# Difference attention's heads kept unnormalised to its end, normalised by tokens beside the output projection; modulation blocks summed in halves

## What is computed

```python
# first block: four heads of difference attention, four of gated linear attention
p = softmax(s)                                   # two softmaxes per head, 64 features each
a = p[:, :, 0] - lam * p[:, :, 1]
da = rmsnorm(einsum(a, v), da_subln_w) * (1 - lam_init)     # norm over the 128 values of a head
go = rmsnorm(gla_bidirectional(...), gla_norm_w) * silu(gr)
h = h + concatenate([da, go]) @ w_out
# second block: both halves of the modulation, 12 blocks of 512 columns
mod, mod_c = silu(c) @ ada_w + ada_b, silu(c_ctx) @ ada_w[:, :2048] + ada_b[:2048]
```

## Time and profile before

| what | us |
|---|---|
| median of three runs | 2268.46 |
| profiled execution | 2262.53 |
| its span | 2261.2 |
| attention, first scores to first product of the output projection | 241.15 to 353.09 |
| output projection, to the residual's last tile on DVE | 353.09 to 395.37 |

### The profile page before, as it was taken

One profiled execution on the slowest core, in us unless ns is written; L12 is line 12 of the kernel. 1 busy time (PEld: TensorE's weight loads), 2 busy tenths in 40 slices (PEclk: granted clock), 3 DMA queues, 4 the chain that ended last, 5 costly groups with the idle time before them and its releaser, 6 DMA issues.

```text
span 2261.2 us, 31215 instructions
## 1 busy us (share of the span) xinstructions
PE 2109.3 (93%) x12667; PEld 1220.4 (54%) x12743; DVE 1524.8 (67%) x2558; ACT 890.9 (39%) x1066; POOL 713.0 (32%) x540
## 2 busy tenths in 40 slices
PE   6999889899999988999999999999789898999998
PEld 5464554455556646666665555555445464444444
DVE  4557664698889899998688888888674374432002
ACT  5333553333333336765433333333232454434110
POOL 2311001310333442232233333434336301555440
PEclk9999889999999999999999999999799998999999
DMA  5223552215988878899999999999422201322410
GB/s 207 75 75 114 197 203 83 84 49 195 330 307 299 333 274 300 332 353 341 372 373 378 376 382 377 382 382 374 174 75 98 75 20 38 112 83 104 149 38 37
DMA packets 194478, 483.37 MB, mean 214 GB/s; under 512 B 10672, under 2 KB 93648, under 8 KB 188320
## 3 DMA queue, kind: packets, MB, share of 16 engines
q1 hardware_dynamic: 154624, 334.65, 41.5%
q0 software_dynamic: 39712, 146.74, 17.2%
HBM read 428.92 MB, written 52.43 MB: 213 GB/s over the span
## 4 chain that ended last, share of the span: by engine, by line
PE 48%; DVE 29%; DMA 14%; issue 3%; ACT 3%; POOL 1%; SPq 1%; DVEq 0%; ACTq 0%; POOLq 0%
PE psum L565 13%; PE psum L566 13%; PE psum L564 13%; DMA expert_act<-act_dram 12%; DVE weight_low L2003 6%; DVE row_sum L2232 2%; POOL weight_low L2565 1%; DVE hidden_low L2411 1%; DVE gated_one_hot_b L2391 1%; DVE one_hot_b L2388 1%; DVE one_hot_a L2385 1%; DVE expert_act L2406 1%; DVE rows_a L2219 1%; PE psum L758 1%; PE psum L779 1%
## 5 line engine op out<-in xcount | busy, mean ns | idle before, releaser
L564 PE MATMUL psum<-x_high,weight_high 128*128 128x384 bf16 (+3 forms) x1826 | 630.0, 345 | 21.1 <-DVE weight_low L2003 15.7
L565 PE MATMUL psum<-x_low,weight_high 128*128 128x384 bf16 (+3 forms) x1845 | 637.2, 345 | 12.1 <-DVE x_low L1881 5.9
L566 PE MATMUL psum<-x_high,weight_low 128*128 128x384 bf16 (+3 forms) x1844 | 636.5, 345 | 0.6
L1289 ACT ACTIVATE weight_high<-weight_stage 128x4096 bf16<-128x4096 f32 (+2 forms) x100 | 356.3, 3564 | 240.8 <-PE psum L566 118.1
L2565 POOL TENSOR_TENSOR weight_low<-weight_stage,weight_high 128x512 bf16<-128x512 f32 (+1 forms) x229 | 299.5, 1341 | 422.7 <-ACT weight_high L1289 422.7
L564 PE MATMUL psum<-hidden_high,weight_high 128*128 128x384 bf16 x1024 | 333.8, 326 | 6.3 <-DVE hidden_low L2411 6.2
L566 PE MATMUL psum<-hidden_high,weight_low 128*128 128x384 bf16 x1024 | 333.8, 326 | 0.0
L565 PE MATMUL psum<-hidden_low,weight_high 128*128 128x384 bf16 x1024 | 333.8, 326 | 0.0
L2003 DVE TENSOR_TENSOR weight_low<-weight_stage,weight_high 128x4096 bf16<-128x4096 f32 x69 | 304.6, 4416 | 11.0 <-ACT weight_high L1289 11.0
L564 PEld LDWEIGHTS psum<-x_high,weight_high 128*128 128x128 bf16 (+1 forms) x1856 | 183.3, 99 | 183.1 <-issue 20.5
L566 PEld LDWEIGHTS psum<-x_high,weight_low 128*128 128x128 bf16 (+1 forms) x1856 | 183.4, 99 | 154.1 <-issue 7.0
(11 more groups left out here) (350 smaller groups left out, 2926.3 us busy)
## 6 DMA issues: line engine op xcount, KB each, us to landing
weight_stage<-peer_u_dram SPq DMA_DIRECT2D x32, 2048.0 KB
weight_stage<-peer_v_dram SPq DMA_DIRECT2D x32, 2048.0 KB
weight_stage<-mlp_w_dram SPq DMA_DIRECT2D x16, 2048.0 KB
weight_stage<-ada_w_dram SPq DMA_DIRECT2D x12, 2048.0 KB
act_dram<-norm_value SPq DMA_DIRECT2D x128, 192.0 KB
gate_dram<-gate_matrices SPq DMA_DIRECT2D x12, 2048.0 KB, 9.9
gates<-gate_dram SPq DMA_DIRECT2D x32, 768.0 KB
expert_act<-act_dram SPq DMA_DIRECT2D x32, 768.0 KB
```

What stands on the lines that cost most here:

```text
L564: self.nc.tensor.matmul(out, left[0], right[0], start=first, stop=False)
L565: self.nc.tensor.matmul(out, left[0], right[1], start=False, stop=False)
L566: return self.nc.tensor.matmul(out, left[1], right[0], start=False, stop=last)
L1289: nc.scalar.activation(k.block_view(m.w_high, n % SPLITS, n), k.block_view(m.w_stage, n % STAGES, n), ACT.Copy).then_inc(*s.w_high.up(n))
```

## The change

1. Difference-attention heads are copied from PSUM into four buffers and squared into buffers of linear attention that are free by then. Nothing else is done to them within the steps.
2. After the steps all four are normalised inside `mixer_out`. The sums of squares are taken with the squares as the stationary operand and two columns of ones (`token_sums`), so each token's sum is one value on one partition: 16 matmuls of two columns. One root of 128 x 16 values, one reciprocal of 128 x 16, then 16 matmuls of 128 columns spread them (`head_spread`), and DVE multiplies from PSUM.
3. `mixer_out` sums the four linear-attention features for tiles 0 to 3, with the sums of squares after tiles 0 and 1 and the spreads after tile 2; then the four difference-attention features for these tiles; then tiles 4 to 7 whole.
4. Linear-attention heads 2 and 3 are normalised in the same way, by 128 x 8 values, in steps 0 to 3.
5. Modulation blocks 4 to 9 are multiplied in halves of four matmuls in steps 4 to 15, blocks 10 and 11 whole in steps 16 and 17, the last turn is in step 18. Turns use bank 5, the sums bank 7.
6. The table of roots is loaded in step 16 (`root_table`).

```diff
 def ada_step(n):
-    g = ADA_LATE + n // 2
-    return (g - 1, None) if n % 2 == 0 and g <= 12 else (None, g) if n % 2 and g < 12 else (None, None)
+    if n == 0:
+        return ADA_LATE - 1, None, ()
+    if 4 <= n < 16:
+        g, half = ADA_LATE + (n - 4) // 2, n % 2
+        return g - 1 if half == 0 and g > ADA_LATE else None, g, (half,)
+    if n >= 16:
+        return (n - 7, n - 6, (0, 1)) if n < 18 else (n - 7, None, ())
+    return None, None, ()
...
 # PE
+    def token_sums(self, heads, stage, first, end, bank):
...
+        for h in range(first, end):
+            nc.tensor.wait_ge(*s.squared.at(stage, h))
+            square = k.head_square(stage, h)
+            for x in range(QT):
+                at = 2 * (QT * (h - self.first_head) + x)
+                ins = nc.tensor.matmul(k.psum[:, bank, at:at + 2], square[:, P * x:P * (x + 1)], self.m.ones[:, 0:2],
+                                       start=True, stop=True)
+        ins.then_inc(*s.square_sum.up(heads, end - 1))
+
+    def head_spread(self, stage, h, roots, bank):
...
+        for x in range(QT):
+            ins = nc.tensor.matmul(k.psum[:, bank, P * x:P * (x + 1)], roots[:, x:x + 1].to_broadcast([P, P]),
+                                   self.m.ident[:, :], start=True, stop=True)
+        ins.then_inc(*s.spread.up(stage, h))
...
-            part = gla_norm_part(GLA_SLOTS + n)
-            if part and part[1] == 1:
-                self.head_sum(("gla_head", part[0]), (7,))
-            part = da_norm_part(n, 1)
-            if part and part[1] == 1:
-                self.head_sum(("da_head", part[0]), (7,))
+            if n == 1:
+                self.token_sums("gla_heads", "gla_head", 2, GLA_HEADS, 7)
+            if n == 2:
+                nc.tensor.wait_ge(*s.inverted.at("gla_heads"))
+                for p in range(2):
+                    self.head_spread("gla_head", 2 + p, m.gla_roots[:, p, :], 6 + p)
             if n >= 3:
                 applying(n - 3)
-            turn, block = ada_step(n)
-            if turn is not None or block is not None:
-                self.modulation(turn, block, (7,))
+            turn, block, halves = ada_step(n)
+            if turn is not None:
+                self.modulation_turn(turn, (5,))
+            if block is not None:
+                self.modulation_sums(block, halves, (7,))
...
-        for t in range(6):
+        for t in range(4):
             banks.append(self.take(("w_out", t), (s.added, ("w_out", t)), (t,)))
-            part(t, order[:-1])
+            part(t, order[:4])
+            if t == 0:
+                self.token_sums("da_heads", "da_head", 0, DA_HEADS - 1, 7)
             if t == 1:
-                self.head_sum(("da_head", DA_HEADS - 1), (7,))
-        for t in range(6):
-            part(t, order[-1:])
-        for t in range(6, KT):
+                self.token_sums("da_heads", "da_head", DA_HEADS - 1, DA_HEADS, 7)
+            if t == 2:
+                self.nc.tensor.wait_ge(*s.inverted.at("da_heads"))
+                for h in range(DA_HEADS):
+                    self.head_spread("da_head", h, m.da_roots[:, h, :], 4 + h)
+        for t in range(4):
+            part(t, order[4:])
+        for t in range(4, KT):
...
 # ACT
+            if n >= 7 and n % QT == 3:
+                square(n // QT - 1)
             if n >= 3:
                 head(n - 3)
-            _, block = ada_step(n)
-            if block is not None:
+            _, block, halves = ada_step(n)
+            if 1 in halves:
                 self.modulation(block)
-        for part in range(5):
-            self.head_norm("da_head", DA_HEADS - 1, part)
+            if n == n_steps:
+                self.root_table("da_heads")
+        square(DA_HEADS - 1)
+        self.head_roots("da_heads", m.da_roots[:, :, :], DA_HEADS - 1)
+        for h in range(DA_HEADS):
+            self.head_high("da_head", h)
...
 # DVE
+        self.head_roots("da_heads", m.da_roots[:, :, :])
+        for h in range(DA_HEADS + 1):
+            if h < DA_HEADS:
+                o = m.da_o[:, h, :]
+                nc.vector.wait_ge(*s.spread.at("da_head", h))
+                nc.vector.scalar_tensor_tensor(o, o, m.da_gain[:, 0:1], k.tile_bank(("da_head", h, "spread")), ALU.mult,
+                                               ALU.mult).then_inc(*s.normed.up("da_head", h))
+            if h > 0:
+                self.head_low("da_head", h - 1)
         self.modulation_gains()
```

More of the change, by code:

```diff
@@ L729, in head_sum @@
         nc, s, k = self.nc, self.s, self.k
[L730 to L731 removed]
         i = self.take(event, (s.rooted, event), banks)
         nc.tensor.wait_ge(*s.squared.at(*event))
[L734 to L748 removed]
+        nc.tensor.matmul(k.bank(i), self.m.ones[:, :], self.m.head_sq[:, :], start=True, stop=True).then_inc(
+            *s.square_sum.up(*event))
@@ new lines, in token_sums @@
+    def token_sums(self, heads, stage, first, end, bank):
+        nc, s, k = self.nc, self.s, self.k
+        if (heads, "sums") not in k.bank_of:
+            self.free_bank(bank, (s.rooted, (heads,)))
+            k.bank_of[heads, "sums"] = bank
+            self.first_head = first
+        for h in range(first, end):
[6 more added lines that the diff above has]
+        ins.then_inc(*s.square_sum.up(heads, end - 1))
@@ new lines, in head_spread, with modulation_turn @@
+    def head_spread(self, stage, h, roots, bank):
+        nc, s, k = self.nc, self.s, self.k
+        self.free_bank(bank, (s.normed, (stage, h)))
+        k.bank_of[stage, h, "spread"] = bank
+        for x in range(QT):
+            ins = nc.tensor.matmul(k.psum[:, bank, P * x:P * (x + 1)], roots[:, x:x + 1].to_broadcast([P, P]),
+                                   self.m.ident[:, :], start=True, stop=True)
+        ins.then_inc(*s.spread.up(stage, h))
+    def modulation_turn(self, turn, banks):
+        nc, s, k, m = self.nc, self.s, self.k, self.m
+        nc.tensor.wait_ge(*s.mod_copied.at(turn))
+        i = self.take(("mod_turn", turn), (s.mod_added, (turn,)), banks)
+        for f in range(4):
+            ins = nc.tensor.matmul(k.psum[:, i, 2 * f:2 * f + 2], m.mod_rows[:, P * f:P * (f + 1)],
+                                   m.strip_sum[:, :], start=True, stop=True)
+        ins.then_inc(*s.mod_turned.up(turn))
@@ L1324, in run, with root_table @@
         self.norm("final2", lambda t: s.added.at("mlp", t))
+    def root_table(self, j):
+        nc, s, m = self.nc, self.s, self.m
+        if s.root_loaded.count:
+            nc.scalar.wait_ge(*s.root_loaded.now())
+        nc.scalar.activation(m.root[:, 12:13], m.eps[:, 0:1], ACT.Sqrt).then_inc(*s.root_loaded.up(j))
     def norm(self, j, ready, parts_free=None):
@@ L1330, in norm @@
         buffers, x, n, _, _, shift, store = k.norm(j)
-        if s.root_loaded.count:
-            nc.scalar.wait_ge(*s.root_loaded.now())
-        nc.scalar.activation(m.root[:, 12:13], m.eps[:, 0:1], ACT.Sqrt).then_inc(*s.root_loaded.up(j))
+        self.root_table(j)
         for t in range(KT):
@@ L2036, in head_norm @@
         if part == 2:
[L2037 to L2048 removed]
+            nc.vector.wait_ge(*s.inverted.at("gla_head", h))
@@ new lines, in head_roots, with head_low @@
+    def head_roots(self, heads, roots):
+        nc, s = self.nc, self.s
+        nc.vector.wait_ge(*s.rooted.at(heads))
+        nc.vector.reciprocal(roots, roots).then_inc(*s.inverted.up(heads))
+    def head_low(self, stage, h):
+        nc, s, m = self.nc, self.s, self.m
+        nc.vector.wait_ge(*s.x_high.at(stage, h))
+        src, dst = (m.da_o[:, h, :], h) if stage == "da_head" else (m.h[:, h, :], DA_HEADS + h)
+        nc.vector.tensor_tensor(m.x_low[:, dst, 0:SEQ], src, m.x_high[:, dst, 0:SEQ], ALU.subtract).then_inc(
+            *s.x_low.up(stage, h))
```

177 lines of the change are left out of this document (79 added, 98 removed).

## The result

The changed kernel takes 2256.15 us (median of five runs, 2253.01 to 2258.88) against 2268.70 (2267.76 to 2270.31): ratio 0.9942, 95% interval 0.9928 to 0.9957. Run once more beside other kernels it took 2251.37 (six runs) against 2267.11: 0.9932, 0.9918 to 0.9946. The forecast was 2254.0, range 2247 to 2262. The two profiled executions differ by 9.5 us, 2253.01 against 2262.53, where the prediction had 14.5 (2248.0). Inside them, the last tile of the residual after the output projection is written at 380.97 instead of 395.37, 14.4 us earlier; the forecast was 14.5.

A forecast was written before the change was run, and what follows sets the result against it. PE was taken to bound the kernel, with 48% of the chain of waits. The attention's gain of 22.1 us less the projection's loss of 7.6 gave 14.5 us less: median 2268.5 to 2254, range 2247 to 2262.

The forecast's parts named there:

- What bounds: Whole kernel: PE holds 48% of the chain of waits; in the attention it stands still for 17.7 of 112.1 us.
- Opening: Attention steps 1 to 5: eight two-column sums and eight spreads replace a head sum; scores(6) at 272.7, gain 6.2 us.
- Steps 6 to 15: Attention: no head sum, table load or long reciprocal; five step pairs of 9.03 us end at 317.9, halved blocks costing nothing.
- Steps 16 to 18: Attention's end: a turn waits behind the table load until 325.8; attention ends at 331.0 against 353.09, its gain 22.1 us.
- The drain of a table load: Step 17: the skill page adds about 1.38 us per table switch, making the gain 13; the trace does not show it.
- Output projection: After the attention: two-column matmuls add 3.9 us, spreads 4.5, a removed head sum saves 0.9; stage 49.9, loss 7.6 us.
- The cover: Output projection: 9.0 us of PE work hides the rest of the normalisation; without it PE would wait DVE's 6 us.
- The rule weighed against the trace: Output projection: the page says busy PE keeps its clock, the trace suggests two-column streaks don't; 2.9 us kept in range.
- A: Opening and projection: clock back early, sums and spreads cheaper; gain 20, 2248.5 us; chance 0.15.
- B: Attention's steps: DVE and ACT set the odd steps, 2.8 us more, plus projection clock drop 2.9; gain 9, 2259.5; chance 0.20.
- C: Later stages: attention is shorter but their transfers do not start earlier; gain under 4, 2267 us; chance 0.07.
- D: Projection: the two-column streak sends PE to 1.2 GHz and it stays; slower from 29 us low, up to 2295; chance 0.04.

The follow-up runs named there:

- experiment 1: Kernel before with only the last two linear-attention heads normed by tokens, modulation blocks left in odd steps from 1: 2267.17 us against 2267.33, ratio 1.000.
- experiments 4 and 7: 4: changed kernel, blocks 4 to 9 whole in odd steps, 2250.68 us; 7: changed kernel, blocks whole and early, no early load, block 5 in step 4, 2246.71 us.
- experiment 8: Changed kernel with 36 more two-column matmuls in the output projection, 48 in a row instead of 12: 2269.9 us, ratio 1.001.
- experiment 6: Changed kernel with modulation blocks whole in odd steps 1 to 15 and no early load of the root's table: 2251.17 us, ratio 0.9933.

## Why the prediction was right, step by step

- **What bounds.** Right. Every microsecond of the gain up to the projection is PE's: 14.6 us of idle time, and 6.0 of busy time.
- **Opening.** Forecast scores(6) at 272.7, measured 271.35. The token sums took 3.5 us (3.3 said), the wait for the roots 0.65 (1.3), the spreads 3.71 (4.2). Scores and transposes of step 2 took 3.4, not 2.5: the row that gave 2.5 was read as one at the low clock, but its granted clock is 1.00 up to the transposes. The step that failed there is step 3, put at the low clock and at 5.1 us; the clock was back behind the spreads, and it took 3.4 (258.31 to 261.68). Steps 4 and 5 took 9.7 with their waits, not 9.1. The mechanism held, the 1.35 us are what these misses leave. But the gain isn't the opening's own (experiment 1): with the blocks left in steps 1 and 3 and the old heads behind it, the token norms alone gave nothing.
- **Steps 6 to 15.** Forecast 45.2 us without halves costing anything. Measured 45.9 (271.35 to 317.27). The step that failed is "halving the blocks does not change this sum": two halves take 1.99 us, not 1.85.
- **Steps 16 to 18.** The turn was put at 325.8 and started at 325.49; the wait behind the table load was the right mechanism. The step that failed is block 11 at 1.85 us: the clock fell behind the wait, and it took 3.45. With a wait of 0.35 for DVE in step 16 the three steps took 15.2 us, not 13.1, and the attention ended at 332.5, not 331.0.
- **The drain of a table load**, which the Trainium skill ("ScalarE: Activation LUTs", What ACT_TABLE_LOAD costs) puts at about 1.38 us: the load begins 0.01 us after the copy ahead of it ends, and the record behind it starts 1.30 us after the 1.28 us load began, at once. Taking the load out gave 2.6 us, but the rows give 0.95 of it to the wait and 1.60 to the clock; nothing is left for a drain.
- **Output projection.** Forecast 49.9, measured 48.5. Both prices were too high: 0.217 instead of 0.245 for two columns (0.5 us in all) and 0.223 instead of 0.28 for a spread (0.9). The cover held: the last `x_low` ended at 350.2 and PE never waited.
- **The rule weighed against the trace.** The earlier trace rows pointed the right way: the two-column streak doesn't hold the clock. At twelve in a row it fell in 2 of the 10 profiles with that streak (experiments 4 and 7) at 1.6 to 1.8 us, less than the 2.9 allowed; at 48 it fell and cost 6.9.
- **Rivals.** A: its cheap spreads came, its clock in the opening came only behind the spreads, except without the early load and in experiment 8. B: only its clock part is real. C: some 3 us are missing up to the gates in the profiles, at least in part by the clock of PE in the gates' stage; the medians don't show them. D: its trigger is real, its point of decision (29 us at the low level) far off.

The sum came out at 14.5 against 14.4 by luck, by errors that cancel: 1.35 and 1.4 us too dear in the opening and the projection, 0.7 and 2.1 us too cheap in the pairs and from step 16 on. The median was measured 2.2 us above the forecast in the first set and 2.6 below it in the second, and the profiled execution 5.0 above. Two ends of the range don't follow from their terms by 1.3 to 1.5 us: A adds up to 2248.5 and not 2247, and B with the dearest spreads to 2263.3 and not 2262. Neither decides anything here.

## What to carry to other kernels

Cost a short wait on PE at its length plus what runs slow behind it: here a wait of 0.95 us cost 2.6 and one of 2.82 in experiment 6 cost 5.5 (2.7 of it behind the wait), so a table load or a bank held on another engine is worth moving even where its own wait looks small. Price each edit in the company it will have: one that gained nothing alone removed a wait that another edit had made the last one. And compare variants by a fixed stretch around the edit, which here repeated to 0.2 us where the whole time moved by 5.

## What was not expected of the hardware

- A PE that the profile shows as busy can lose its clock: 48 float32 matmuls of two columns in a row, 3.00 us busy in every 3.00, ran at 0.217 us each and then at 0.43 (5.12 us for twelve).
- Whether a given wait brings the clock down differs between kernels with the same instructions around it (1.92 or 3.64 us for the same block behind the same 2.82 us wait), but repeated within 0.2 us of A+B in each of the three kernels profiled twice.
- Eight modulation sums in one piece (16 records) cost 1.85 us, and cut in two 1.99, with nothing between the halves but other matmuls.
